# Memory projections of both layers inside the selecting stage of a two-layer hybrid decoder step

## The reference

```python
for l in range(2):
    yp = mixer(rmsnorm(xp, g[0]))                  # l=0: gated short conv beside sparse attention
    xp = xp + rmsnorm(yp, g[1])
    mk, mv = mem_kv(mem_prompt, mem_norm_g[l], w_xk[l], w_xv[l])   # both are outputs too
    xp = xp + rmsnorm(cross_attend(rmsnorm(xp, g[2]), mk, mv, w_xq[l], w_xo[l]), g[3])
    xp = xp + rmsnorm(sq_relu_mlp(rmsnorm(xp, g[4]), w_ff1[l], w_ff2[l]), g[5])

def mem_kv(mem, g, w_k, w_v):                      # mem is (256, 1024), w_k and w_v are (1024, 512)
    mn = rmsnorm(mem, g)
    return (mn @ w_k).reshape(..., 4, 128), (mn @ w_v).reshape(..., 4, 128)
```

## Time and profile before

| | us |
|---|---|
| median of 3 timed runs | 4152.63 |
| the runs | 4151.81 to 4155.01 |
| the profiled execution's own time | 4149.72 |
| span of the profile, first to last instruction | 4147.9 |
| PE busy | 3489.6 (84% of the span) |
| DVE busy | 1850.8 (45%) |
| ACT busy | 1413.5 (34%) |
| POOL busy | 122.1 (3%) |
| DMA moved | 336.41 MB, 81 GB/s in the mean |

### The profile page before, as it was taken

How to read it: one execution, slowest core, us unless ns; L and a number is a source line. 1 busy time by engine, 2 the same in 40 slices (tenths; PEclk the granted TensorE clock), 3 DMA queues, 4 the chain that set the end, 5 groups by cost and what they waited for, 6 DMA issues and landing times. The chain is left out here.

```text
span 4147.9 us, 44334 instructions
## 1 busy us (share of the span) xinstructions
PE 3489.6 (84%) x17383; PEld 2749.7 (66%) x17383; DVE 1850.8 (45%) x3239; ACT 1413.5 (34%) x2340; POOL 122.1 (3%) x136
## 2 busy tenths in 40 slices
PE   5869943987968799999997998686578889999997
PEld 4734632534747699899786764474456779989886
DVE  3556998601323544444543310442622544444444
ACT  4442113631333433433444310221323443343443
POOL 0002110023000000000000000000000000000000
PEclk9989976998979899999998999655789989999998
DMA  2003100045122333333441100001212143333353
GB/s 75 24 23 101 36 1 0 1 138 193 46 81 82 112 123 122 122 122 123 146 138 36 46 26 22 1 1 23 66 51 81 57 132 132 128 121 123 112 163 113
DMA packets 223089, 336.41 MB, mean 81 GB/s; under 512 B 33205, under 2 KB 161821, under 8 KB 222882
## 3 DMA queue, kind: packets, MB, share of 16 engines
q1 hardware_dynamic: 211106, 291.63, 21.7%
q0 software_dynamic: 11776, 41.95, 3.0%
HBM read 323.06 MB, written 10.19 MB: 80 GB/s over the span
## 5 line engine op out<-in xcount | busy, mean ns | idle before, releaser
L198 PE MATMUL ps<-s_mlp_xl,s_mlp_w1h 128*128 128x384 f32 (+1 forms) x1536 | 499.5, 325 | 9.5 <-DVE s_mlp_xl L603 9.5
L200 PE MATMUL ps<-s_mlp_xh,s_mlp_w1h 128*128 128x384 f32 (+1 forms) x1536 | 496.0, 323 | 0.0
L199 PE MATMUL ps<-s_mlp_xh,s_mlp_w1l 128*128 128x384 f32 (+1 forms) x1536 | 495.5, 323 | 0.0
L585 DVE TENSOR_TENSOR s_mlp_w2l<-s_mlp_w2b,s_mlp_w2h 128x1024 fp32r<-128x1024 f32 x192 | 235.0, 1225 | 583.0 <-ACT s_mlp_w2h L471 583.0
L198 PE MATMUL ps<-s_mlp_w2l,s_mlp_hh 128*128 128x512 f32 x1024 | 405.0, 395 | 20.5 <-DVE s_mlp_hl L622 16.2
L199 PE MATMUL ps<-s_mlp_w2h,s_mlp_hl 128*128 128x512 f32 x1024 | 403.0, 394 | 0.0
L200 PE MATMUL ps<-s_mlp_w2h,s_mlp_hh 128*128 128x512 f32 x1024 | 402.5, 393 | 0.0
L471 ACT CAST s_mlp_w2h<-s_mlp_w2b 128x1024 fp32r<-128x1024 f32 x192 | 201.2, 1049 | 586.7 <-PE ps L200 586.6
L198 PEld LDWEIGHTS ps<-s_mlp_xl,s_mlp_w1h 128*128 128x128 f32 x1536 | 289.7, 189 | 41.4 <-issue 35.2
L199 PEld LDWEIGHTS ps<-s_mlp_xh,s_mlp_w1l 128*128 128x128 f32 x1536 | 289.7, 189 | 6.2
L200 PEld LDWEIGHTS ps<-s_mlp_xh,s_mlp_w1h 128*128 128x128 f32 x1536 | 289.5, 188 | 0.0
(11 more groups left out here) (504 smaller groups left out, 6087.1 us busy)
## 6 DMA issues: line engine op xcount, KB each, us to landing
s_mlp_w1b<-w_ff SPq DMA_DIRECT2D x96, 1024.0 KB, 6.1
s_mlp_w2b<-w_ff SPq DMA_DIRECT2D x96, 1024.0 KB, 8.4
x_kb<-cache_mem_k SPq DMA_DIRECT2D x16, 512.0 KB, 6.9
x_vb<-cache_mem_v SPq DMA_DIRECT2D x2, 4096.0 KB, 20.7
s_orows_raw<-w_in_odd SPq DMA_DIRECT2D x32, 256.0 KB, 3.0
s_convsel_w<-w_in_even SPq DMA_DIRECT2D x12, 512.0 KB, 3.9
x<-x_prompt SPq DMA_DIRECT2D x1, 4096.0 KB, 12.7
ev_mixT<-w_in_even SPq DMA_DIRECT2D x16, 256.0 KB, 3.3
```

The lines of the kernel that those rows point to most:

```text
L198: nc.tensor.matmul(out, ah, bl, start=first, stop=False, skip_group_check=True)
L199: nc.tensor.matmul(out, al, bh, start=False, stop=False, skip_group_check=True)
L200: return nc.tensor.matmul(out, ah, bh, start=False, stop=last, skip_group_check=True)
L585: nc.vector.tensor_tensor(w2l[:, s % RING], w2b[:, c % 3, s % FC, :], w2h.bitcast(F32)[:, s % RING], ALU.subtract).then_inc(low2, 1)
```

## The change

- The 18 moves of `stage_pick` go into `stage_index`, on SP, with the clearing on POOL; `stage_pick` is gone.
- `stage_load_mem`, the norm of the memory tiles and `stage_mem_rows` are gone for both layers. Their work is in `stage_conv_select`, once for both layers: the memory tokens are loaded and normalised once (ACT squares and scales, DVE two small operations), PE transposes them in four groups at rounds 8, 14, 20 and 24, ACT applies the two layers' gains, and PE forms the four products (two layers, keys and values) in rounds 25 to 32, four weight slices of 256 KB per round, from a ring of four slices.
- All of that lives in the tile `G.x`. `stage_attend` loads the residual again from the inputs.
- Keys and values of memory are stored to their outputs in `stage_conv_select` and loaded back in `stage_turned_split`, which also transposes the keys between its sixth and seventh units.
- The sample mask is written in the order in which `stage_sample_attend` needs it; the last four columns are written by an instruction of their own.

```diff
+        @block.gpsimd
+        def _(pool):
+            nc.gpsimd.memset(A.qs[:], 0.0).then_inc(blank, 1)
+
+        @block.sync
+        def _(sp):
+            for half in range(2):
+                o = 64 * half
+                for par in range(2):
+                    sp.dma_start(A.qi[o:o + 64, par:par + 7:2, :], B.qiT[64 * par:64 * par + 64, :, SEQ:TOK]).then_inc(moved, 16)
+                sp.dma_start(A.kis[o:o + 64, :], B.kT[o:o + 64, 2, SEQ:TOK]).then_inc(moved, 16)
+            for b in range(DB):
+                sp.dma_start(A.vnew[:, b, :], A.vrow[DS * b:DS * b + DS, NT, :]).then_inc(moved, 16)
+            sp.wait_ge(blank, 1)
+            for kv in range(2):
+                for par in range(2):
+                    sp.dma_start(A.qs[64 * kv:64 * kv + 64, 4 * kv + par:4 * kv + par + 3:2, :],
+                                 B.qT[64 * par:64 * par + 64, 2 * kv:2 * kv + 2, SEQ:TOK]).then_inc(moved, 16)
+            sp.wait_ge(moved, 16 * 18)
...
+        spare = G.x.rearrange("p t d -> p (t d)")
+        mem = spare[:, 0:2 * D].rearrange("p (a d) -> p a d", a=2)
+        m_out = spare[:, 0:2 * D].rearrange("p (s a n) -> p s a n", s=2, a=2)
+        memT = spare[:, 2 * D:6 * D].rearrange("p (l k m) -> p l k m", l=2, k=KD)
+        m_w = spare[:, 6 * D:8 * D].rearrange("p (s n) -> p s n", s=4)
+        m_junk = spare[:, 8 * D:9 * D]
+        m_stat = G.stat[:, NT + 1:NT + 3]
+        m_root = S.sb("m_root", [P, 2])
+        m_gain = S.sb("m_gain", [P, 2, KD])
+        m_mats = [(l, n, wn) for l in range(2) for n, wn in (("mem_k_p", "w_xk"), ("mem_v_p", "w_xv"))]
+        TURN_AT = (8, 14, 20, 24)
+        FIRST = 25
...
+            def store_mem(m):
+                l, name, _ = m_mats[m]
+                sp.wait_ge(m_kept, 2 * m + 2)
+                sp.dma_start(G.o[name][l, 0].rearrange("(a p) h e -> p a (h e)", p=P), m_out[:, m % 2]).then_inc(m_stored[m % 2], 16)
...
+                if q == 1:
+                    sp.dma_start(mem, G.d["mem_prompt"][0].rearrange("(a p) d -> p a d", p=P)).then_inc(mem_in, 16)
+                    for l in range(2):
+                        sp.dma_start(m_gain[:, l, :], G.d["mem_norm_g"][l].rearrange("(k p) -> p k", p=P),
+                                     allow_slow_non_contiguous=True).then_inc(mem_in, 16)
+            for q in range(4 * KD):
+                m, k = divmod(q, KD)
+                if k == 0 and m >= 2:
+                    store_mem(m - 2)
+                if q >= 4:
+                    sp.wait_ge(m_used, q - 3)
+                sp.dma_start(m_w[:, q % 4], G.d[m_mats[m][2]][m_mats[m][0]][k * P:(k + 1) * P, :]).then_inc(m_w_in[q % 4], 16)
...
+            def turn_mem(b):
+                if b == 0:
+                    pe.wait_ge(m_scaled, 2)
+                else:
+                    pe.wait_ge(m_gained, 4 * b)
+                for k in range(2):
+                    for a in range(2):
+                        ins = nc.tensor.transpose(G.ps[:, 7, (2 * k + a) * P:(2 * k + a + 1) * P],
+                                                  mem[:, a, (2 * b + k) * P:(2 * b + k + 1) * P], G.ident[:])
+                ins.then_inc(m_turned, 1)
+
+            def mem_product(q):
+                m, k = divmod(q, KD)
+                if q == 0:
+                    pe.wait_ge(m_gained, 16)
+                    for s in (u_kept, z_made, gb_kept):
+                        pe.wait_ge(s, 12)
+                if k == 0 and m >= 2:
+                    pe.wait_ge(m_kept, 2 * m - 2)
+                pe.wait_ge(m_w_in[q % 4], 16 * (q // 4 + 1))
+                for a in range(2):
+                    ins = nc.tensor.matmul(G.ps[:, 2 * (m % 2) + a, :], memT[:, m_mats[m][0], k, a * P:(a + 1) * P], m_w[:, q % 4, :],
+                                           start=(k == 0), stop=(k == KD - 1))
+                ins.then_inc(m_used, 1)
...
+                if x in TURN_AT:
+                    turn_mem(TURN_AT.index(x))
+                if x >= FIRST:
+                    for q in range(4 * (x - FIRST), min(4 * (x - FIRST) + 4, 4 * KD)):
+                        mem_product(q)
...
+            def gain_mem(b):
+                act.wait_ge(m_turned, b + 1)
+                for k in range(2):
+                    for l in range(2):
+                        kk = 2 * b + k
+                        nc.scalar.activation(memT[:, l, kk, :], G.ps[:, 7, 2 * k * P:(2 * k + 2) * P], ACT.Copy,
+                                             scale=m_gain[:, l, kk:kk + 1]).then_inc(m_gained, 1)
+
+            def keep_mem(m):
+                act.wait_ge(m_used, KD * (m + 1))
+                if m >= 2:
+                    act.wait_ge(m_stored[m % 2], 16)
+                for a in range(2):
+                    nc.scalar.copy(m_out[:, m % 2, a, :], G.ps[:, 2 * (m % 2) + a, :]).then_inc(m_kept, 1)
+
+            act.wait_ge(mem_in, 48)
+            for a in range(2):
+                if a:
+                    act.wait_ge(m_squared, 1)
+                nc.scalar.activation(m_junk, mem[:, a, :], ACT.Square, accum_out=m_stat[:, a:a + 1]).then_inc(m_squared, 1)
...
+                    if n == 0 and j == 2:
+                        act.wait_ge(m_meaned, 1)
+                        nc.scalar.activation(m_root[:], m_stat, ACT.Sqrt).then_inc(m_rooted, 1)
+                    if n >= 1 and j == 2:
+                        gain_mem(n - 1)
...
+                if n == 0:
+                    act.wait_ge(m_inverted, 1)
+                    for a in range(2):
+                        nc.scalar.activation(mem[:, a, :], mem[:, a, :], ACT.Copy, scale=m_stat[:, a:a + 1]).then_inc(m_scaled, 1)
...
+            gain_mem(3)
+            for m in range(3):
+                keep_mem(m)
             act.wait_ge(tail_turned, 1)
             nc.scalar.copy(tail_rows, G.ps[0:18, 7, :]).then_inc(tail_kept, 1)
+            keep_mem(3)
...
+                if x == 1:
+                    dve.wait_ge(m_squared, 2)
+                    nc.vector.tensor_scalar(m_stat, m_stat, 1.0 / D, EPS, ALU.mult, ALU.add).then_inc(m_meaned, 1)
+                if x == 3:
+                    dve.wait_ge(m_rooted, 1)
+                    nc.vector.reciprocal(m_stat, m_root[:]).then_inc(m_inverted, 1)
...
+                if sample:
+                    chain.add(nc.vector.tensor_scalar(dst[:, 0:SEQ].rearrange("p (j q) -> p q j", j=8),
+                                                      cum[:, 0:SEQ].rearrange("p (q j) -> p q j", j=8), -1.0, -NEG, ALU.add, ALU.mult))
+                    dst, cum, wd = dst[:, SEQ:W], cum[:, SEQ:W], DS
...
+            sp.dma_start(G.x[:, 0:NT, :], G.d["x_prompt"].rearrange("b (t p) d -> p (b t) d", p=P)).then_inc(loaded, 16)
+            sp.dma_start(G.x[0:NS, NT, :], G.d["x_sample"].rearrange("b t d -> (b t) d")).then_inc(loaded, 16)
+            sp.wait_ge(loaded, 32)
...
-                keys = C.sc[:, 0:SEQ].rearrange("p (q j) -> p j q", j=8)
+                keys = C.sc[:, 0:SEQ].rearrange("p (j q) -> p j q", j=8)
...
+        seq = [divmod(i, 3) for i in range(6)] + [("keys", 0), ("keys", 1)] + [divmod(i, 3) for i in range(6, 3 * tiles)]
...
+                if n == 1:
+                    sp.dma_start(mk[:], G.o["mem_k_p"][l, 0].rearrange("(a p) h e -> p a (h e)", p=P)).then_inc(keys_in, 16)
+                    sp.dma_start(X.mv[:], G.o["mem_v_p"][l, 0].rearrange("(a p) h e -> p a (h e)", p=P)).then_inc(values_in, 16)
+            sp.wait_ge(values_in, 16)
...
+                if n == "keys":
+                    if c == 0:
+                        pe.wait_ge(keys_in, 16)
+                    for h in range(HX):
+                        ins = nc.tensor.transpose(G.ps[:, i % 8, h * P:(h + 1) * P], mk[:, c, h * P:(h + 1) * P], G.ident[:])
+                    ins.then_inc(product, 1)
+                    continue
...
+                if n == "keys":
+                    nc.scalar.copy(X.mkT[:, :, c * P:(c + 1) * P], G.ps[:, i % 8, :].rearrange("p (h m) -> p h m", h=HX)).then_inc(kept, 1)
+                    continue
...
-            stage_pick(nc, G, A, B)
...
-        with ExitStack() as cm:
-            X.mem = cm.enter_context(nc.sbuf_tensor(f"x{l}_mem", [P, 2, D], F32))
-            stage_load_mem(nc, G, X, l)
-            stage_norm(nc, G, f"nm{l}", X.mem, [P, P], d["mem_norm_g"][l], G.xnT, at=NT + 1)
-        stage_mem_rows(nc, G, X, l)
```

More of the change, by code:

```diff
@@ L994, in stage_conv_select @@
         seg = S.sb("seg", [P, 2, P])
+        spare = G.x.rearrange("p t d -> p (t d)")
[10 more added lines that the diff above has]
+        FIRST = 25
+        mem_in, m_squared, m_meaned, m_rooted, m_inverted, m_scaled, m_turned, m_gained, m_used, m_kept = (
+            S.sem(x) for x in ("mem_in", "m_squared", "m_meaned", "m_rooted", "m_inverted", "m_scaled", "m_turned", "m_gained",
+                               "m_used", "m_kept"))
+        m_w_in = [S.sem(f"m_w_in{i}") for i in range(4)]
+        m_stored = [S.sem(f"m_stored{i}") for i in range(2)]
         w_ready = [S.sem(f"w_ready{i}") for i in range(4)]
```

(34 more changed lines are left out.)

65 lines of the change are left out of this document (11 added, 54 removed).

## The result

The changed kernel takes 4014.3 us (median of 4 runs, 4012.4 to 4018.8) against 4152.2 us (4149.8 to 4155.0): a ratio of 0.967, 95% interval 0.965 to 0.969, or 137.9 us less. The forecast was 140.9 us less.

A forecast was written before the change was run, and what follows sets the result against it. Stages run one after another, with PE or DVE nearly full in the key windows; -128.4 - 16.0 + 0.9 + 0.2 + 2.1 + 0.3 = -140.9 us from 4152.63 gives 4011.7 us, range 4006 to 4018, widened to 4004 to 4029.

The forecast's parts named there:

- Memory stages and moves: Removing stage_pick and both layers' memory stages takes 14.25 + 56.87 + 57.24 = 128.36 us off the path.
- Rounds 25 to 31: Selecting stage, second half: four slices and the sum fit under DVE's 7.20 us round, with 3 us of room; cost 0.
- (b): Weight ring late in the selecting stage: 7 us from freed slot to landing, total 4018 us; chance 0.09.
- (c): PE stays at the lower clock in rounds 25 to 31: +43 us, total 4055; chance 0.03.
- (d): Slower than before, possible only through the weight ring at 7.0 us a slice; chance 0.02, half of it slower.
- Rounds 0 to 24: Selecting stage, first half: PE's transposing groups and DVE's two small operations add 0.2 us, bounds 0 and +2.
- Mask order: Sample attention's key loop: contiguous mask reads save 2.0 us in each of eight sets, 16.0 us; bounds 0 and 16.
- rival (a): The mask gain in the sample attention does not arrive: total 4028 us; chance 0.08.
- Sample mask write: End of the selecting stage: DVE's strided write and four remaining columns add 0.9 us, bounds +0.2 and +1.5.
- Query projection: PE is full there, so eight key transposes per layer add 2.1 us for both layers; bounds 0 and +3.
- Reload: Reloading the 4 MB residual under the 164.10 us attention stage without DMA costs 0; uncovered 12.7 us.
- semaphores: Extra POOL clearings before the cached index keys and cached keys add 0.3 us, bounds 0 and +0.5.

The follow-up runs named there:

- The run with five slices: Changed kernel with five weight slices of the memory products in each of rounds 25 to 30 and two in round 31, instead of four each; 4017.7 us (one run).
- the run with the keys early: Changed kernel with projected-memory loads moved into the norm stage and key transposes put ahead of the query projection's first product; 4011.1 us.

## Why the prediction held, point by point

The large terms held by their mechanism. That the sum came out within 3 us (5 us for the profiled executions) is in part luck: five terms of the account were missed to the same side, by 0.5 to 2.2 us, the 2.3 us of the value loop were not in the sum, and the -2.7 us of stages that the change doesn't touch offset part of this.

- **Memory stages and moves (-128.4).** Right to 0.9 us. Both memory stages gave back their whole length (56.9 and 57.2 us), since what moved lies under DVE's rounds. The index stage became 0.8 us longer because PE's clock rose later; this was not in the sum.
- **Rounds 25 to 31 (0).** Right: 3 us of room forecast at the first sum, 2.1 measured, a round 7.09 us on PE against 7.20. The missing us is the cold start, taken as 1.55 us from the earlier trace rows: the first four slices took 9.84 us, 2.73 more than the next, with a granted clock of 0.50 until 568 us. The run with five slices shows the edge. Rivals (b) and (c), the late ring and the lower clock, and with them (d), are out: no wait for a slice, and slices of 256 KB landed in 2.7 us; PE takes 7.11 us for four slices from the second group on, and only the first took 9.84.
- **Rounds 0 to 24 (+0.2).** The step that listed what DVE and PE would wait for there was right, and its cost is nothing (178.57 against 178.59). The size was wrong, +1.3 us, because POOL was taken to have room by its busy share: what counts is whether one of its operations runs when DVE's short list comes. The trace of before showed this already (485.14, 2.29 us).
- **Mask order (-16.0).** The mechanism was right, rival (a) is out, the term too large. That each of the eight sets gives 2.0 us holds for six; the masks of the first and the fifth run near or partly at the lower clock in five of the seven profiles with the new order, and in the changed kernel's they gave 1.0 and 0.4 us. The keys were 137.4 us on average in three profiles with the old order and 123.3 in seven with the new: 14.1. Net of the write, for which the forecast is 15.1, the times say 14.1 and 15.0.
- **Sample mask write (+0.9).** +0.57 us, inside the bounds. The two pages of the Trainium skill that were weighed gave, by the prediction's estimate, +1.5 (Advanced Engine Details and Errata, section SBUF Cachelines) and +0.2 (VectorE: DVE Perf Modes, section What auto-detection actually checks); 1.24 us against 0.70 agrees with neither.
- **Query projection (+2.1).** In the changed kernel's profile the two layers took +0.75 and +2.4 us. The products' time multiplied by their granted clock tells the transposes from the clock: it is about 45.9 us before, 46.7 in the changed kernel and 46.0 with the transposes ahead, in both layers. So the transposes cost some 0.8 us a layer, 1.6 us of the 2.1. The rest is PE's clock and first products that start 0.9 and 0.6 us later after the norm's start; why these start later was not traced.
- **Reload (0), semaphores (+0.3).** The attention lasts no longer. The first gather of the cached index keys is 0.16 us later for its two semaphores (not with the moves in a stage of their own), half of what was assumed for each. The half us more up to the first round's sum was not traced further.
- **Left open.** The value loop of the sample attention spread from 51.9 to 55.7 us over ten profiles, in step with no edit. PE waits there for gathers, POOL for buffers that PE frees, and DVE for PE; what makes one execution faster was not found. What decides whether PE's clock falls in the 2.02 us wait, and in which of the two stages behind the norm it is lower, was not tried.

## What to carry to other kernels

Work moves for nothing under an engine that has a fixed pace, as long as what that engine waits for stays ahead of the pace: count the round, not the share. Before calling DVE the pace, look for short DVE operations that end together with a POOL operation; waits that keep POOL's long operations off DVE's serial list took two lines here and gave 5.7 us. A saving on PE is to be counted at the clock that the place has: behind a wait it may be much smaller, and what one stage gains can be lost in the next at a lower clock, as in the run with the keys early, so the stage behind belongs in the count.

## What the runs showed of the hardware that was not expected

- Short DVE operations (128x7, 0.17 us) took 1.0 to 2.3 us beside POOL's additions and products of two SBUF operands, with nearly the same lengths in every profile with the same code in this stage, and 0.17 us when POOL was held back. DVE counts of 128x384 to 128x1028 with an accumulator ran beside them unhindered.
- A mask read 32 bytes apart took PE nearly the same time whatever the granted clock (3.75 us at 1.00, 3.84 at 0.69 and at 0.60), the contiguous mask 1.92 at 1.00 and 3.49 at 0.54.
- After the same wait of 2.02 us the granted clock of the contiguous mask was 0.53 to 0.54 in five profiles and 1.00 in two, and it was 1.00 in the 5 us ahead of the wait in all of them.
